# Two neighbouring PSUM banks filled matmul by matmul in turn, in both MLPs of a two-block transformer kernel

## What is computed

```python
h = rms_norm(x, norm_mlp[l])
x = x + jnp.square(jax.nn.relu(h @ w_up[l])) @ w_down[l]
...
return rms_norm(x, norm_final)

n2 = rms_norm_2(h, norm_mlp_pre[l])
hid = jnp.square(jax.nn.relu(jnp.einsum('bsd,df->bsf', n2, w_up[l])))
mlp_out = jnp.einsum('bsf,fd->bsd', hid, w_down[l])
h = h + rms_norm_2(mlp_out, norm_mlp_post[l])
```

## Time and profile before

| | |
|---|---|
| Median of 3 runs | 1682.95 us (1681.89 to 1683.21) |
| Span of the profiled execution | 1682.1 us |
| PE busy in the span | 1626.1 us (97%) |
| PE weight loads | 1350.5 us (80%) |
| DVE busy | 848.4 us (50%) |
| ACT busy | 604.7 us (36%) |
| POOL busy | 85.5 us (5%) |
| Mean granted TensorE clock | 0.989 |

### The profile page before, as it was taken

How to read it: one execution, slowest core, us unless ns; L and a number is a source line. 1 busy time by engine, 2 the same in 40 slices (tenths; PEclk the granted TensorE clock), 3 DMA queues, 4 the chain that set the end, 5 groups by cost and what they waited for, 6 DMA issues and landing times.

```text
span 1682.1 us, 20235 instructions
## 1 busy us (share of the span) xinstructions
PE 1626.1 (97%) x7742; PEld 1350.5 (80%) x7742; DVE 848.4 (50%) x1059; ACT 604.7 (36%) x985; POOL 85.5 (5%) x76
## 2 busy tenths in 40 slices
PE   6999999999999999999899999999999899999997
PEld 5688788877678888888788898988888788888885
DVE  4364556444354444444555646457354744444444
ACT  5342344243243332232343334454323533333331
POOL 2332000000000000000000000010011000000001
PEclk9999999999999999999999999999999999999998
DMA  5222213421223223323222222243323232333231
GB/s 220 63 76 76 76 51 101 163 77 51 92 88 100 90 98 100 97 90 100 88 87 81 71 76 88 79 146 117 101 88 97 92 101 92 96 100 99 89 99 50
DMA packets 43221, 157.39 MB, mean 94 GB/s; under 512 B 5064, under 2 KB 5408, under 8 KB 42768
## 3 DMA queue, kind: packets, MB, share of 16 engines
q1 hardware_dynamic: 40176, 144.89, 27.2%
q0 software_dynamic: 2976, 11.54, 1.9%
HBM read 154.23 MB, written 2.18 MB: 93 GB/s over the span
## 4 chain that ended last, share of the span: by engine, by line
PE 89%; DVE 5%; ACT 3%; DMA 1%; issue 1%; POOL 1%; SPq 0%; POOLq 0%; DVEq 0%; ACTq 0%
PE banks L833 27%; PE banks L834 26%; PE banks L835 26%; DVE w_lo L1326 1%; PE banks L988 1%; PE banks L1070 1%; PE banks L1000 1%; PE banks L1021 1%; PE banks L1039 1%; PE banks L936 1%; PE banks L1010 1%; PE banks L902 1%; DMA w_first<-in_weights 1%; PE banks L979 1%; PE banks L1051 1%
## 5 line engine op out<-in xcount | busy, mean ns | idle before, releaser
L1326 DVE TENSOR_TENSOR w_lo<-w_raw,w_hi 128x1024 fp32r<-128x1024 f32 x264 | 331.8, 1259 | 183.9 <-ACT w_hi L1108 174.8
L833 PE MATMUL banks<-act_hi,w_hi 128*128 128x512 f32 x1024 | 403.6, 394 | 7.5 <-DVE act_lo L1410 7.0
L1108 ACT ACTIVATE w_hi<-w_raw 128x1024 fp32r<-128x1024 f32 x264 | 276.5, 1055 | 350.2 <-PE banks L835 181.8
L835 PE MATMUL banks<-act_hi,w_lo 128*128 128x512 f32 x1024 | 399.9, 390 | 0.0
L834 PE MATMUL banks<-act_lo,w_hi 128*128 128x512 f32 x1024 | 399.8, 390 | 0.0
L833 PE MATMUL banks<-w_hi,mid_hi 128*128 128x512 f32 x640 | 249.6, 390 | 1.2 <-DVE mid_lo L1410 1.2
L835 PE MATMUL banks<-w_hi,mid_lo 128*128 128x512 f32 x640 | 249.1, 389 | 0.0
L834 PE MATMUL banks<-w_lo,mid_hi 128*128 128x512 f32 x640 | 249.1, 389 | 0.0
L833 PEld LDWEIGHTS banks<-act_hi,w_hi 128*128 128x128 f32 x1024 | 192.9, 188 | 50.2 <-DVE act_lo L1410 8.1
L835 PEld LDWEIGHTS banks<-act_hi,w_lo 128*128 128x128 f32 x1024 | 192.9, 188 | 40.2
L834 PEld LDWEIGHTS banks<-act_lo,w_hi 128*128 128x128 f32 x1024 | 193.0, 188 | 39.0
(11 more groups left out here) (284 smaller groups left out, 1583.6 us busy)
## 6 DMA issues: line engine op xcount, KB each, us to landing
w_raw<-in_weights SPq DMA_DIRECT2D x264, 512.0 KB, 3.5
wide<-share_dram POOLq DMA_DIRECT2D x3, 1024.0 KB, 7.8
x_tok<-in_x SPq DMA_DIRECT2D x4, 512.0 KB, 5.0
w_first<-in_weights SPq DMA_DIRECT2D x4, 512.0 KB, 11.7
x_tok<-in_x POOLq DMA_DIRECT2D x1, 2048.0 KB, 10.4
out<-x_tok SPq DMA_DIRECT2D x4, 512.0 KB, 2.6
near_back<-bias_dram POOLq DMA_DIRECT2D x1, 1024.0 KB, 7.4
mem_tok<-in_mem POOLq DMA_DIRECT2D x1, 1024.0 KB, 6.7
```

What stands on the lines that cost most here:

```text
L833: pe.matmul(out_ap, lhs[0], rhs[0], start=start, stop=False)
L835: return pe.matmul(out_ap, lhs[1], rhs[0], start=False, stop=stop)
L1108: act.activation(w_hi[:, t % 8, :], landed(t), ACT.Copy).then_inc(hi_w, 1)
L1326: dve.tensor_tensor(w_lo[:, t % 8, :], landed(t), w_hi[:, t % 8, :], ALU.subtract).then_inc(lo_w, 1)
```

## The change

In all groups of both MLPs the steps of banks 0 and 1 are joined, and those of banks 2 and 3. `bank_steps` marks the step of the even bank as "first" and gives the odd one a reference to it. `gemm` returns at once for the even step; at the odd step it waits for both banks, then runs over k, and for each k over the three parts, with one matmul for the even bank and one for the odd bank each time. Each bank signals its own last matmul. ACT, DVE, POOL and SP run the same lists of instructions in the same order as before. The number of matmuls, weight loads and signals is the same. Since `work(tt)` comes after every step in the list, but only in the queues of the other engines, PE's order is changed by the pairing alone.

```diff
@@ bank_steps
+            if paired and b % 2 == 0:
+                st.pair, even = "first", st
+            elif paired:
+                st.pair = even
@@ run_mlp
-            s.gemm("up", "T", "act", ready=act_ready, mid=c % 2)
+            s.gemm("up", "T", "act", ready=act_ready, mid=c % 2, paired=True)
...
-            s.gemm("add", "tok", "mid", rows=4, halves=2, ready=mid_ready, mid=c % 2, dst=dst)
+            s.gemm("add", "tok", "mid", rows=4, halves=2, ready=mid_ready, mid=c % 2, dst=dst, paired=True)
...
-        steps = s.bank_steps("add", "tok", "mid", rows=4, halves=2, ready=odd, mid=1, dst=dst)
+        steps = s.bank_steps("add", "tok", "mid", rows=4, halves=2, ready=odd, mid=1, dst=dst, paired=True)
@@ gemm on PE
             def gemm(st, turn):
-                begin(st.bank, st.fill[0], turn)
+
+                if st.pair == "first":
+                    return
+                for one in ([st] if st.pair is None else [st.pair, st]):
+                    begin(one.bank, one.fill[0], turn)
+                if st.after == "yb" and st.half == 0 and st.bank == 0:
+                    pe.wait_ge(yb_split, 1)
+                for k in range(st.rows):
+                    pair = [(one, *operands(one, k, turn)) for one in ([st] if st.pair is None else [st.pair, st])]
+                    for part, (i, j) in enumerate(((0, 0), (0, 1), (1, 0))):
+                        for one, out_ap, lhs, rhs in pair:
+                            last = k == st.rows - 1 and part == 2
+                            mm = pe.matmul(out_ap, lhs[i], rhs[j], start=k == 0 and part == 0, stop=last)
+                            if last:
+                                mm.then_inc(bank_done[one.bank], 1)
```

More of the change, by code:

```diff
@@ L119, in __init__ @@
                  after=None, tiles=TT, gains=(), chunks=(), row=None, row_n=0, qk_ready=None,
-                 of=None, roped=None, packed=None, rstd=None, xn=None, hi=None, xrows=None, smax=None, merged=None, relu=None):
+                 of=None, pair=None, roped=None, packed=None, rstd=None, xn=None, hi=None, xrows=None, smax=None, merged=None, relu=None):
         self.kind, self.banks, self.fill = kind, banks, fill
@@ L128, in __init__ @@
         self.of = of
+        self.pair = pair
         self.roped, self.packed, self.rstd, self.xn, self.hi, self.xrows, self.smax, self.merged, self.relu = (
@@ L196, in bank_steps @@
     def bank_steps(self, out, major, src, rows=KC, banks=4, halves=1, ready=None, blk=0, mid=None, dst=None, p=None,
-             after=None):
+             after=None, paired=False):
         g = self.group
@@ L843, in gemm, with operands @@
+            def operands(st, k, turn):
                 set_at = 4 * (st.tile[0] // 4 % 2)
                 b = st.bank
[L845 to L872, removed]
@@ L873, in gemm @@
-                mm.then_inc(bank_done[b], 1)
+                tile = k // 2 + st.half * (st.rows // 2)
+                if st.first and k % 2 == 0:
+                    pe.wait_ge(lo_w, at(st.tile, turn, tile + 1))
+                if st.ready is not None:
+                    wait_ready(pe, st.ready[k:k + 1], turn)
+                if st.src == "mid":
+                    n = k // 4 if st.mid is None else st.mid
+                    act = (mid_hi[n][:, k % 4, :], mid_lo[n][:, k % 4, :])
+                elif st.src == "memT":
+                    act = (mem_hi[:, k, :], mem_lo[:, k, :])
+                else:
+                    act = (act_hi[:, k, :], act_lo[:, k, :])
@@ new lines, in operands @@
+                w = [x_[:, set_at + tile, (k % 2) * 512:(k % 2) * 512 + 512] for x_ in (w_hi, w_lo)]
+                if st.major == "T":
+                    n = M if st.src == "memT" else T
+                    return psum[:, b, 0:n], [x_[:, b * P:b * P + P] for x_ in w], act
+                if st.out == "v2" and st.p > 0:
+                    act = [x_.rearrange("q (m r) -> q r m", r=4)[:, b, :] for x_ in act]
+                else:
+                    act = [x_[:, b * P:b * P + P] for x_ in act]
@@ L875, in handle @@
+                return psum[:, b, :], act, w
             def handle(st, turn):
```

## The result

The changed kernel takes 1689.85 us (median of 5 runs, 1687.62 to 1690.69) against 1683.21 for the kernel before, run beside it: a ratio of 1.0040, 95% interval 1.0029 to 1.0051, so 6.7 us more (interval 4.9 to 8.6). Where a ratio and the two medians beside it differ a little, this text goes by the ratio and its interval. The time lies inside the forecast range of 1684.0 to 1694.0, 2.2 us above the forecast of 1687.6, and within rival A's 1684.5 to 1690.5. The profiled execution took 1690.69 us with a span of 1688.9, 6.8 us longer than the span before.

What follows compares the result with a forecast made beforehand. The prediction took PE's matmul rate to bound the kernel (PE busy 97% of the span). Terms 0 + 0 + 1.2 + 1.4 + 0.3 + 1.8 = 4.7 us, with span 1682.1 and 0.85 around it, gave 1687.6; range 1684.0 to 1694.0.

Steps and rivals of the forecast that it cites:

- rival A: Whole kernel: the summed terms hold and the rhythm doesn't feel a change of bank; 1684.5 to 1690.5 us, chance 0.60.
- Part 1: Inside the MLPs: alternating banks makes the 3072 matmuls neither shorter nor longer; zero, bounds 3 us either way.
- rival C: Inside the MLPs: neighbours in one bank cost PE 13 ns a matmul; if all went, 41 us less, 1647; chance 0.09.
- Part 2: Hand-overs between groups, tightest from up to down, 14 in all: banks come free later, slack 0.3 us, cost zero.
- X+5.33: Up-to-down hand-over: bank 3's mid_lo over 5.33 us after X, the start of bank 2's last matmul.
- Rival B: Up-to-down hand-over: PE waits for bank 3's mid_lo 14 times, 0.2 to 0.6 us each; 5.6 us more, 1693; chance 0.14.
- Part 3: Start of each MLP: the first pair also waits for bank 1, so for chunk 1; +0.6 us each, +1.2.
- Part 4: End of the first MLP: bank 0 finishes later, delaying ACT's series and bank 2's add; +1.4 us, plus a clock term.
- the 0.3 for the clock: Behind the first MLP and at the second's start together: low clock falling on matmuls; 0.3 us, bounds 0 and 1.6.
- Part 5: End of the second MLP: bank 0's later add delays row products and POOL's adds; +1.8 us, bounds 1.0 and 2.7.
- Sum: Whole kernel: 0 + 0 + 1.2 + 1.4 + 0.3 + 1.8 = 4.7 us more, forecast 1687.6 us.
- the four terms of the ends: MLP starts and ends: +0.6 us at each start, +1.4 at the first MLP's end, +1.8 at the second's.

Runs made afterwards that it cites:

- the two squares: Two unused DVE squares ahead of bank 3's in each up group: on the changed kernel 1701.41 us (1.0111), on the kernel before 1683.09 (1.0000).
- fillers: Extra PE matmuls in the gap behind the first MLP and between transposes, also before the second MLP: changed kernel 1686.48 us (1.0015), kernel before 1681.92 (0.9988).

## Why the prediction was right, point by point

**Part 1, no shorter matmul: right.** 348.05 and 348.02 us for 1536 matmuls against 348.07 and 348.06, so at most 0.03 ns a matmul. The boundary of banks in the trace before had said it. The 13 ns above 512 columns that rival C made its own are there with alternating banks too; what they are stays open. The Trainium skill ("TensorE: Matmul & The Clock Gate", the part on the gap between matmuls) has 215.7 ns from start to start; the 34 us that this figure would have given if the bank were the cause did not come, and the starts stayed 226.7 ns apart.

**Part 2, the tight hand-over: right, the end of mid_lo to 0.02 us.** The sum had bank 3's mid_lo end at X+5.33, which is 4.88 after down's first matmul; it ended 4.86 after it, in 14 of 14 hand-overs within 0.02. DVE in the changed kernel:

```profile
707.80 1.23 DVE L1341 TENSOR_TENSOR w_lo<-w_raw,w_hi 128x1024 fp32r<-128x1024 f32 x1
708.95 0.69 DVE L1370 TENSOR_TENSOR square<-relu 128x512 f32<-128x512 f32 x1
709.75 0.69 DVE L1373 TENSOR_TENSOR mid_lo<-square,mid_hi 128x512 fp32r<-128x512 f32 x1
```

The slack was summed against PE's weight load (0.3 us); with the two squares it comes out as 0.43. Rival B did not happen; the two squares show what it would have cost. With its 14 waits of 0.6 us, 44 us apart, no low stretch began inside either MLP (the one at the start of the second had begun before it), so the further loss by a falling clock did not appear.

**Part 3, the starts: right.** +0.61 and +0.62 for +0.6 each.

**Part 4, the end of the first MLP: right in its main term, wrong in the clock.** +1.28 in gap 1 for +1.4; the first transpose behind the MLP stands 5.29 us behind the last matmul instead of 3.91, +1.38, and 0.1 came back later. The step that failed in size is the 0.3 for the clock: it was 2.07 in the profiled execution, above the bound of 1.6 that I had given. I had bounded it by half of the 3.1 us of low clock between 844 and 848. The same stretch had begun at 840.3, while PE waited and transposed, and was 6.8 us long; half of that, 3.4, would have been a bound that holds. The window rows of the kernel before that I left out of it:

```profile
840.00:842.00 2.00, 0.91 (x5) 0.83 (x5) 1.27 (x3) 1.94 (x6) 0.00 (x0) 0.57 0.00 0
842.00:844.00 2.00, 1.14 (x6) 0.73 (x4) 1.75 (x2) 1.94 (x5) 0.57 (x1) 0.50 0.04 8
```
In the changed kernel there were two stretches, one at 841.2 and one at 848.0 (0.85 in 844 to 846 and 1.00 in 846 to 848 between them), and the second fell wholly on the transposes and the first eleven matmuls. The loss isn't bound to this place: in other executions it fell on the start of the second MLP, and by the table above the change adds 1.2 us of it in the mean, by the medians with fillers 2.2, both uncertain.

**Part 5, the end of the second MLP: right.** +1.68 for +1.8, by the steps named: POOL's second and third adds move with the row products.

The last DVE add ended 6.8 us later in the span, not 4.5: 4.2 are the ends', 2.1 the clock's, and some 0.5 lie in other stages.

**Sum.** The difference was forecast as 4.7 and measured as 6.7 us. The ends gave 4.2 for 4.4. By the two profiles the clock gave 2.1 for 0.3, and 0.4 came from stages ahead of the change, for which there was no term and which the change doesn't touch; that part is scatter between executions. The last 0.3 of the 2.2 us by which 1687.6 was low is that the kernel before took 1683.21 us beside the changed one, not 1682.95. The mechanism and the four terms of the ends were right; that the whole came within 2.2 us owes something to which stretches the clock happened to fall in, since that alone moved single executions by up to 2.5 us.

## What to carry to other kernels

When two streams are joined so that they finish together, ask three things: who waits for both at the start, who was using the earlier finish at the end, and how much slack is left to free the later buffer; the steady state between may be free to the last nanosecond. Where the path at a stage's end runs through other engines, look there for work that isn't needed yet (here a weight split between two tiles' statistics): moving it won 3 us (0.9973 to 0.9991), while the order of PE's matmuls won nothing. And a term for a clock that falls in idle times should be bounded by the whole of a low stretch as seen, not by the part of it that lies beside work today: the change moves the work, and the stretch with it.

## What the runs showed of the hardware

PE's clock falls to the low level after idle times and may do so again between short bursts: the low stretches stood in other places from profile to profile (350.01 us for an MLP that otherwise takes 348.06, 23.96 for 96 matmuls that take 21.89). Filling one gap removed one stretch and left the next; only when the idle times between the transposes were filled too did both places stay at 1.00, in both kernels. Transposes between idle times did not keep it up: with the gap filled, the next stretch began at 846.6, behind three bursts of transposes of 1.1 to 1.3 us with 1.1 and 1.9 us of idle time between them. Matmuls that follow the low level start 0.427 us apart until it rises, and the row's length (0.63 for 0.39) shows it. A wait that ends too late costs its lateness: PE's matmul starts 0.15 us after the end of the DVE instruction it waits for, and the matmul behind it comes about 0.08 later than the rhythm (14 of 14 hand-overs in the kernel with the two squares).
